# FFN's first product by seven products for eight, rotary repacked, and half of a tile's projection put off

## What is computed

```
h  = h + rms_norm(merged @ w_out, g_mix_post)
hn = rms_norm(h, g_ffn_pre)                        # per token: h * rsqrt(mean(h*h)+eps) * g
f_gate, f_up = split(hn @ w_ffn_in)                # 1024 x (2 * 2816)
f  = (silu(f_gate) * f_up) @ w_ffn_out             # 2816 x 1024
h  = h + rms_norm(f, g_ffn_post)
...
layer 0: mix = (silu(g) * group_norm(retention(q, k, v))) @ ret_w_out     # 2048 x 1024
layer 1: MLA; scores of head e = q_nope.k_nope + q_rope.k_rope            # 128 and 64 wide, k_rope shared by heads
         softmax, values, @ mla_w_out
each layer: h = layer_norm(ALPHA*h + mix)
            peer_ffn(h): top 16 of product keys per head, gather u and v of 16 experts per token and head
            h = layer_norm(ALPHA*h + ffn)
```

## Time and profile before

| | us |
|---|---|
| median of 3 runs | 2361.03 |
| lowest, highest | 2359.1, 2362.63 |
| profiled execution | 2363.76 |
| its span in the trace | 2362.0 |
| w_out, 330 to 365 | TensorE busy 33.42 of 35 |
| norms ahead of the FFN, 365 to 383 | TensorE busy 11.65 of 18 |
| FFN first product, 383 to 537 | TensorE busy 153.55 of 154, VectorE 10.02 |
| peer of layer 0, 932 to 1570 | DMA engines busy all the time, 417 GB/s |
| MLA with its projections, 1570 to 1720 | TensorE busy 144.20 of 150 |
| peer of layer 1, 1720 to 2362 | DMA share 0.99, 412 GB/s |

### The profile page before, as it was taken

How to read it: one execution, slowest core, us unless ns; L and a number is a source line. 1 busy time by engine, 2 the same in 40 slices (tenths; PEclk the granted TensorE clock), 3 DMA queues, 4 the chain that set the end, 5 groups by cost and what they waited for, 6 DMA issues and landing times.

```text
span 2362.0 us, 23326 instructions
## 1 busy us (share of the span) xinstructions
PE 2137.4 (90%) x7050; PEld 1289.5 (55%) x7050; DVE 1203.4 (51%) x2896; ACT 685.9 (29%) x1490; POOL 617.3 (26%) x545
## 2 busy tenths in 40 slices
PE   9999998999999999999887788889999998887876
PEld 8868887888884845444442222258644443322222
DVE  3983113000250036666666666634466666666674
ACT  1112101100110113343444343433243444343442
POOL 0210000000000002444444444400144555444442
PEclk9999999999999999999999999999999999999999
DMA  5444342444354326999999999973499999999997
GB/s 221 145 158 154 141 151 99 160 143 154 132 222 151 141 91 277 421 421 421 421 422 421 421 422 422 422 324 107 173 421 421 421 422 422 422 421 422 422 422 320
DMA packets 97992, 702.55 MB, mean 297 GB/s; under 512 B 11008, under 2 KB 11264, under 8 KB 12800
## 3 DMA queue, kind: packets, MB, share of 16 engines
q0 software_dynamic: 73728, 536.90, 54.7%
q1 hardware_dynamic: 21168, 149.43, 17.5%
q10 hardware_dynamic: 3024, 15.27, 1.7%
HBM read 700.51 MB, written 1.05 MB: 297 GB/s over the span
## 4 chain that ended last, share of the span: by engine, by line
PE 55%; DMA 31%; ACT 5%; issue 5%; DVE 3%; POOL 0%; DVEq 0%; POOLq 0%; ACTq 0%
DMA arena<-uv,expert_index 31%; PE acc L431 30%; PE aux L773 11%; PE acc L459 4%; PE aux L627 3%; PE acc L695 2%; ACT arena L1198 1%; ACT arena L1201 1%; PE acc L783 1%; ACT L1198 1%; ACT L1190 1%; DVE arena L1774 1%; DVE arena L1399 1%; POOL arena L971 0%; PE acc L672 0%
## 5 line engine op out<-in xcount | busy, mean ns | idle before, releaser
L773 PE MATMUL aux<-arena 128*128 128x512 f32 x2048 | 1007.8, 621 | 187.8 <-ACT arena L1201 182.8
L971 POOL DMA_INDIRECT arena<-uv,expert_index x512 | 591.7, 1156 | 1088.2 <-PE aux L773 619.5
L1774 DVE SCALAR_TENSOR_TENSOR arena<-arena 128x1024 f32<-128x1024 f32 x512 | 633.4, 1237 | 428.3 <-DMA arena<-uv,expert_index 426.8
L773 PEld LDWEIGHTS aux<-arena 128*128 128x128 f32 x2048 | 366.3, 192 | 730.0 <-ACT arena L1201 442.1
L431 PE MATMUL acc<-x,w_ring 128*128 128x256 f32 x2352 | 514.4, 381 | 10.0 <-DVE x L1356 4.8
L431 PEld LDWEIGHTS acc<-x,w_ring 128*128 128x128 f32 x2352 | 449.6, 191 | 73.8 <-issue 6.1
L1198 ACT ACTIVATE arena<-ident,dots 128x128 f32<-128x128 f32 x512 | 205.3, 401 | 705.6 <-DVE arena L1774 703.7
L431 PE MATMUL acc<-arena,w_ring 128*128 128x256 f32 x1032 | 224.3, 379 | 3.7 <-DVE arena L1463 1.6
L431 PEld LDWEIGHTS acc<-arena,w_ring 128*128 128x128 f32 x1032 | 195.7, 190 | 31.7 <-issue 2.6
L1201 ACT ACTIVATE arena<-arena,gate 128x128 f32<-128x128 f32 x512 | 205.5, 401 | 17.0
L957 POOL IOTA arena<- 128x512 int32 x1 | 0.6, 557 | 529.8 <-DVEq L1523 529.8
(11 more groups left out here) (260 smaller groups left out, 1179.2 us busy)
## 6 DMA issues: line engine op xcount, KB each, us to landing
w_ring<-stream SPq DMA_DIRECT2D x141, 1024.0 KB
arena<-uv,expert_index POOLq DMA_INDIRECT x512, 14.9
first_query_weights<-first_heads ACTq DMA_DIRECT2D x4, 1024.0 KB, 14.8
row_vectors<-rows ACTq DMA_DIRECT2D x3, 1024.0 KB, 12.8
scratch<-keys ACTq DMA_DIRECT2D x2, 1024.0 KB, 6.8
x<-first_heads ACTq DMA_DIRECT2D x2, 1024.0 KB, 4.8
arena<-rows ACTq DMA_DIRECT2D x1, 1024.0 KB, 4.7
out<-arena SPq DMA_DIRECT2D x4, 256.0 KB, 5.0
```

The source lines that it names most:

```text
L773: last = nc.tensor.matmul(AUX[2 * tt + c][:, :], DG[:, slot, :], G[:, slot, D + c * 512:D + (c + 1) * 512], start=False, stop=closes)
L971: pool.indirect_dma_start(G[:, s % RING, :], None, uv, bass.IndirectOffsetOnAxis(ap=EIDX[:, par, s:s + 1], axis=0),).then_inc(gathered[s % ...
L1774: v.scalar_tensor_tensor(G[:, slot, 0:D], G[:, slot, 0:D], 1.0, HTM[:, tt, :], ALU.mult, ALU.mult, accum_out=HD[:, slot:slot + 1]).then_in ...
```

## The change

**FFN first product.** The tokens are split in two tiles of 128 and the channels in pairs of tiles; the columns of w_ffn_in are split in gate and up. Each 2x2 block product is made by seven products of 128x128 with 512 columns in place of eight (Strassen in Winograd's form). There are six units of columns (five of 512 gate and 512 up columns, one of 256 each) of four steps (pairs of channel tiles). For each step VectorE makes four sums of weights (`combine`: one instruction of 1024 columns, two of 512) into QW, and once at the start four sums of tokens for each of the four pairs (`split`, 128 columns each). The seven results gather in seven banks over the four steps; VectorE adds them up (`add_products`, seven instructions), ScalarE copies the first and takes silu.
**Norm's factors.** The product starts on h times the gain; the factor of each token is put in behind it, as scale of silu and in the multiplication (`gate_f`). f is then token-major and is turned back by 44 transposes (`turn_f`).
**Projection.** ret_out's first two blocks are loaded apart by ScalarE's queue into the place of QK. Tile 1's c=0, k 0 to 7 are done in `rest`. The rows of G are renamed (`row`), and from the fifth gather on GpSimd waits for `projected`.
**Rotary.** The key is rotated into one tile and masked to two halves; the queries are packed by eight small transfers within SBUF, so that a score has two products, not three.

```diff
-          ("ple_gate", 4), ("ret_qk", 8), ("ret_v", 8), ("ret_g", 8), ("ret_out", 8), ("peer_q0", 5),
+          ("ple_gate", 4), ("ret_qk", 8), ("ret_v", 8), ("ret_g", 8), ("ret_out", 6), ("peer_q0", 5),
...
+        SEVEN = {1: ACC[0], 6: ACC[1], 2: ACC[2], 7: ACC[3], 5: AUX[0], 4: AUX[1], 3: AUX[2]}
...
+        def row(s):
+            return (s + 2) % RING
...
+            def seven_step(unit, j):
...
+                operands = {1: (a11, b[:, 0:w]), 2: (a12, b[:, 3 * w:4 * w]), 3: (s4, b[:, 2 * w:3 * w]),
+                            4: (a22, t4), 5: (s1, t1), 6: (s2, t2), 7: (s3, t3)}
+                if unit == 0:
+                    pe.wait_ge(x_scaled, j + 1)
+                order = (1, 2, 4, 5, 6, 7, 3) if step == 0 else (1, 6, 2, 7, 5, 4, 3)
+                read = {6: 1, 2: 2, 7: 3, 5: 5, 4: 6, 3: 7}
+                for at, q in enumerate(order):
+                    if q == 5 and step == 0 or at == 1 and unit == 0 and j:
+                        pe.wait_ge(split_ready, j + 1)
+                    if q == 4 and step == 0 or at == 1 and step:
+                        pe.wait_ge(combined, step + 1)
+                    if unit and j == 0 and q == 1:
+                        pe.wait_ge(first_copied, unit)
+                    elif unit and j == 0:
+                        pe.wait_ge(banks_read, 7 * (unit - 1) + read[q])
+                    last = nc.tensor.matmul(SEVEN[q][:, 0:w], operands[q][0], operands[q][1],
+                                            start=(j == 0), stop=(j == STEPS - 1))
...
-            idle_products(10)
-            square_sums(per=2)
-            idle_products(10)
-            loop(pairs, 5, X1, KT, 8, need_half)
-            pairs(X1, KT, 4)
-            stored_by_evacuation()
-            pairs_and_sums(F, FT)
+            idle_products(20)
+            n["squares"] += 4
+            for unit in range(FFN_UNITS):
+                for j in range(STEPS):
+                    seven_step(unit, j)
+                    if unit == 0 and j == 1:
+                        token_sums()
+                    if unit and j in (1, 2):
+                        turn_f(unit - 1, j - 1)
...
+            pairs_and_sums(F, FT, need_f_once)
...
-            for k in range(12):
-                last = project(YG, 16, 0, k, 1, out0)
+            for k in range(8, 12):
+                last = project(YG, 16, 0, k, 1, out0, start=(k == 8))
...
-                        last.then_inc(slot_free, RING - 2)
+                        last.then_inc(slot_free, RING)
...
-                pe.sem_inc(slot_free, 2)
...
-            peer(0, YG, 16, out0, [(1, 0), (1, 1)], [(1, k) for k in range(2, 16)])
+            peer(0, YG, 16, out0, [(1, 0), (1, 1)],
+                 [(1, k) for k in range(2, 8)] + [(0, k) for k in range(8)] + [(1, k) for k in range(8, 16)])
...
-            need_input()
+            pe.wait_ge(packed_even, 16 * 4)
+            pe.wait_ge(packed_odd, 16 * 4)
...
-                    nc.tensor.matmul(o, QR[:, e // 4, qt * P:(qt + 1) * P], KRM[:, e % 4, :], start=False, stop=False)
-                    last = nc.tensor.matmul(o, QR[:, 2 + e // 4, qt * P:(qt + 1) * P], KRM[:, 4 + e % 4, :],
+                    last = nc.tensor.matmul(o, QP[:, e // 2, qt * P:(qt + 1) * P], KRM[:, e % 2, :],
...
+            def pack(q):
+                for j in range(2):
+                    at = q % 2 * 64 + j * 32
+                    nc.gpsimd.dma_start(QP[at:at + 32, q // 2:4:2, :], QR[q * 32:q * 32 + 32, 2 * j:2 * j + 2, :])\
+                      .then_inc(packed_even, 16)
...
+                if layer:
+                    pool.wait_ge(rotated, 1)
+                    for q in (0, 2):
+                        pack(q)
...
+                            if par == 0 and s == RING // 2:
+                                pool.wait_ge(projected, TT * (layer + 1))
...
-            squares_by_pair(X0)
-            root(RS)
+            for s in range(4):
+                n["centred"] += 1
+                act.wait_ge(centred, n["centred"])
+                nc.scalar.activation(X1[:, 2 * s, :], X0[:, 2 * s, :], ACT.Copy, scale=col("g_ffn_pre", 2 * s))
...
+            act.wait_ge(scores_ready, RET_HEADS)
+            for b in range(2):
+                act.dma_start(HELDW[:, b, :, :], ret_out_held[b]).then_inc(held_loaded, 16)
...
+            def combine(step):
...
+                dve.wait_ge(w_full[b % SLOTS], 16 * (b // SLOTS + 1))
+                if step >= 2:
+                    dve.wait_ge(steps_done, step - 1)
...
+                link(v.tensor_tensor(t13, x[:, w:3 * w], x[:, 0:2 * w], ALU.subtract))
+                link(v.tensor_tensor(t2, x[:, 2 * w:3 * w], t1, ALU.subtract))
+                v.tensor_tensor(t4, x[:, 3 * w:4 * w], t2, ALU.subtract).then_inc(combined, 1)
...
+            copy_out(MO, combine)
+            add_normed("g_mix_post", centred, split)
+            split(STEPS - 1)
+            combine(2)
+            n["squares"] += 4
+            dve.wait_ge(squares_ready, n["squares"])
+            fold(SC)
+            combine(3)
+            sums_done()
...
+            combine(STEPS)
+            add_products(0)
+            for unit in range(1, FFN_UNITS):
+                combine(STEPS * unit + 1)
+                gate_f(unit - 1)
+                combine(STEPS * unit + 2)
+                combine(STEPS * unit + 3)
+                if unit + 1 < FFN_UNITS:
+                    combine(STEPS * (unit + 1))
+                add_products(unit)
+            gate_f(FFN_UNITS - 1)
```

More of the change, by code:

```diff
@@ new lines, in turn_f @@
+            def turn_f(unit, half):
+                pe.wait_ge(f_ready, unit + 1)
+                if unit or half:
+                    pe.wait_ge(f_stored, 2 * unit + half)
+                for c in range(2):
+                    for tt in range(TT):
+                        at = (2 * half + c) * P
+                        last = nc.tensor.transpose(AUX[3][:, c * S + tt * P:c * S + (tt + 1) * P],
+                                                   FTM[:, tt, at:at + P], IDENT[:, :])
+                last.then_inc(f_turned, 1)
@@ L717, in some @@
                         c, k = rest.pop(0)
-                        last = project(x, kt, c, k, 1, b0, k == kt - 1)
-                        q = c * kt + k - (base - b0) * 4
-                        if q % 4 == 3 and q < 15:
+                        last = project(x, kt, c, k, 1, b0, (c, k) not in rest and all(c != other for other, _ in rest),
+                                       start=False if kt == 16 else None)
+                        q = c * kt + k - (kt if kt == 16 else 0)
+                        if q % 4 == 3 and 0 <= q < 15:
                             last.then_inc(w_free[(base + q // 4) % SLOTS], 1)
@@ L1471, in copy_out @@
+            def copy_out(dst, between=None):
                 for s in range(4):
```

242 lines of the change are left out of this document (182 added, 60 removed).

## The result

The changed kernel takes 2326.0 us (median of four executions, 2325.2 to 2329.0), the kernel before 2361.0 beside it (2359.1 to 2362.6): ratio 0.9858, 95% interval [0.9844, 0.9872]. It is 35.0 us faster; the forecast was 2325.3. The profiled execution took 2325.90 (span 2324.2), that of before 2363.76 (span 2362.0). So the two traces differ by 37.8 us, 2.8 more than the medians, most of it because the execution shown of before was 2.7 over its median.

The account below looks back on a forecast made before the run. TensorE was taken to bound the FFN's first product and DMA layer 0's experts. Savings of 26.4 (FFN), 3.9 (projection) and 5.4 (rotary) sum to 35.7 us: 2361.03 - 35.7 = 2325.3, range 2318 to 2341.

Parts of the forecast that it names:

- The FFN's length: FFN's first product on TensorE: 137.5 us of products, transposes and sums, plus 1.1 of waiting; FFN saves 26.4 with its start.
- The wait for the fold: After the FFN's step 1, TensorE waits 1.1 us until VectorE has folded the norm's squares.
- VectorE's cover: In each FFN unit VectorE's 17.2 us of sums, additions and multiplications fit beside TensorE's 24.9, so no product waits.
- The rival: VectorE bounds the FFN; all gain is gone at 31.4 us a unit; chance 0.04, milder form 0.05.
- The start: The FFN's first product starts at 372.85 us, ahead of the norm's factors, where TensorE started it at 382.77 before.
- the product doesn't start ahead of the norm: Rival at the FFN's start: a late entry in VectorE's queue loses the 9.9 us there, giving 2335; chance 0.06.
- The projection: Eight products moved behind layer 0's first gather bring it 6.9 us forward; 3 given back as idle DMA, 3.9 saved.
- the ninth gather: In layer 0's experts it comes 5.1 us later, counted from the first gather, as VectorE norms tile 1 later.
- The rotary part: 16 products of 256 columns fewer in the scores, 6.9 us, less 1.5 of waits: 5.4 saved.
- waits in the heads: In the first heads of scores (0 to 3), some 1.5 us of waits on VectorE and ScalarE appear.
- The packing: Before the scores, the small transfers of queries land at 1628.2 to 1629.8 us, mostly covered; cost taken as 0.
- the half clock: Rival: TensorE runs the whole FFN stage of 137 us at 1.2 GHz, giving 2462; chance 0.02.

Follow-up runs that it names:

- x5: The changed kernel with each of VectorE's sums of weights made twice, the repeat writing the same numbers: 2343.90 us, ratio 0.9932 to the kernel before.
- x6: The changed kernel with each of VectorE's sums of weights made three times: 2398.83 us, ratio 1.0160 to the kernel before.
- x4: The changed kernel with the FFN's first product started only behind the norm's root, fifty idle products for twenty: 2339.80 us, ratio 0.9911 to the kernel before.
- y1: y0 with the put-off half of tile 1's projection taken back ahead of the first gather: 2325.86 us, ratio 0.9856 to the kernel before.
- x1: The changed kernel with the put-off half of tile 1's projection taken back ahead of the first gather: 2325.4 to 2329.6 us, ratio 0.9855 to the kernel before.
- y0: The changed kernel with idle products added in three idle times of TensorE (at 12, 594 and 625 us): 2323.41 us, ratio 0.9844 to the kernel before.
- x7: The changed kernel without the twenty idle products ahead of the FFN: 2329.17 us, ratio 0.9866 to the kernel before.
- a0: The changed kernel run again unchanged, beside the kernel before on the same chip: 2325.85 us, ratio 0.9854.

## Why the prediction was right, step by step

**The FFN's length** was right to half a microsecond: 137.5 + 1.1 forecast, 137.85 measured, as TensorE's products cost per column the same in both forms and don't slow beside VectorE. The wait for the fold is 0.41 for 1.1: VectorE's splits ended at 380.2, not 380.8, and operations that don't depend on each other overlap by 0.08 us. The gain there is 27.35 for 26.4: 0.7 from the fold, 0.35 from the start (372.50 for 372.85; the norm behind w_out was itself 0.3 earlier in that trace, as all since the first product of 16.35 for 16.66).

**VectorE's cover** of 17.2 beside 24.9 us is 16.4 by starts. The rival had its break-even at 31.4 us a unit. x5 and x6 bracket it: at 27.3 the stage is 15.3 us longer, with the sums made three times (38.1 by the same count) 66, so all of the 35.7 is gone at a little over 31, an estimate on the straight line between them. The mechanism was right and its chance rightly small; some 2 us a step are left, enough for one or two more sums, not for a second `combine` (2.71).

**The start.** By x4 the start ahead of the norm is worth 11 to 12 us. The rival "the product doesn't start ahead of the norm" had 9.9 us, counted from the kernel before, where it measures 10.3.

**The projection** was the term that missed, inside its bounds: 6.87 us reach the first gather as forecast, 3.55 are given back where I took 3.0, so 3.3 are saved for 3.9 (2.7 to 2.9 by y1 and x1, which keep the rest of the change). The step that was short is the ninth gather: I put it 5.1 us later against the first, it is 6.9 later. I had taken the delay from the start of VectorE's norm of tile 1, and that start is 5.1 later (16.18 us behind the first gather for 11.06). But the ninth gather waits for the first weighing, that one for ScalarE, and ScalarE for TensorE's products behind the projection, which shift by all eight products: 6.87. The wait through TensorE ends last there, not VectorE's. The place of the idle DMA, gathers 5 to 8 and before the ninth, was right. Layer 1 lost nothing.

**The rotary part** gave 6.13 for 5.4. I had 1.5 us of waits in the heads; there are 0.32 at 1602.67, 0.40 at 1620.84 and 0.17 at 1621.67, and the last is in the kernel before too. TensorE has 3.03 us a head, as forecast. The packing is hidden: GpSimd issued its four transfers in 2.23 us from 1589.42, so the last one landed about 1594 and the scores began at 1598.67. Small transfers landed in 2.5 us from GpSimd's queue and 2.7 from ScalarE's, not in my 4.1 to 5.7. For GpSimd's queue the Trainium skill (DMA: Bandwidth & Descriptors, Anatomy of one DMA) had said 2.0 us plus the bytes, by which 64 KB take 2.15 (an estimate); the trace is 0.35 above it, and much nearer to it than to my rows.

**Sum.** 27.35 + 3.3 + 6.1 = 36.8, and 1.0 in layer 1's experts, which nothing in the change explains, make the 37.8 of the traces. My terms were 1.1 too small (0.95 FFN, 0.7 rotary, less 0.6 projection). The medians differ by 35.0, less than the terms, because the profiled execution of before lay 2.7 over its median and the one after 0.1 under its own. That the forecast of 2325.3 lies only 0.7 from the median is partly luck: the terms were 1.1 too small, and the medians happen to differ by 1.8 less than the terms that the traces show. That executions of one kernel differ through the clock dips of y0's part is shown; that these 2.7 us are of that kind is not.

**The clock.** The forecast gave the half clock 0.02. The granted clock is 1.00 over the stage, and x7, which starts it at the lower level, loses 2.3 us and no more. The Trainium skill (TensorE: Matmul & The Clock Gate, A second HAM failure mode) tells of a clock that swings in a bf16 kernel whose products go round the banks with TensorE idle for short times between groups. This trace has no such idle times (TensorE busy 99.7%) and no swing, so it shows the prediction's reading, that seven banks in turn are that pattern, to be too wide, and does not test the skill's own case.

## What to carry to other kernels

Strassen's seven for eight pays where TensorE is busy throughout, another engine has the room per unit and not only on average, and the norm's factors can stand behind the product: count that engine's dependent operations from start to start, and compare with TensorE's time for the same unit. Work that is moved behind a gate costs nothing only until the queue that it gates runs dry: find the first transfer that then starts late, and move that one, not its successor. An idle time of TensorE of 2 to 3 us cost another 1.7 us in some of these executions; count that, or fill the time.

## What was not expected of the hardware

- The granted clock behind the same idle time of 2.3 to 2.7 us falls in one execution and not in another (0.59 and 1.00 in the stretch 16 to 20 us; near 596, 0.62 in a0 and 1.00 in the first trace), 1.6 to 1.7 us each time; in ten traces it fell nine times behind the first such idle time and four times behind the second. That is of the size of the spread of 2 to 4 us between executions; that it makes the spread is not shown. Experiments that shift TensorE's work are read better from the trace, stage by stage, than from medians.
- A dependent VectorE operation starts 0.04 us after the end of the one before (1.26 behind 1.22, 0.73 behind 0.69), an independent one 0.08 us before it (0.60 behind 0.68).
- Moving a 64 KB tile from partition to partition inside the chip's own memory by DMA landed in 2.5 to 2.7 us (2.4 to 3.0 over all runs), faster than any load from outside in these traces (3.6 us and more).
- With VectorE as the bound and TensorE waiting in every step, TensorE's granted clock is lower too (0.86 in x6, 1.00 in the changed kernel).
